# Sixteen raw weight buffers and four high ones in order of use, loads held until the first gather, one weight split moved ahead of the result copy, and a contiguous gated tile

## The chip, the cores and the metric

The kernel runs on one core of a Trainium2 chip, in one launch. The metric is the device time of one execution in microseconds. Three runs of the kernel before took 1229.41, 1229.84 and 1231.94 us; their median is 1229.84 us. The engines are TensorE (PE for its matmuls, PEld for its weight loads), VectorE (DVE), ScalarE (ACT), GpSimd (POOL) and SyncE (SP). SyncE here only issues transfers; GpSimd issues the gathers and the scatters.

## The reference, cut to what matters

One transformer block over 512 tokens of width 1024, all in fp32: three token mixers (dilated attention, a gated recurrence, attention over a memory), then a mixture of experts. The change touches the second half alone: the router, the shared expert's end and the 64 routed experts. Each token takes 8 experts.

```
u = rmsnorm(x, ffn_norm_g[layer]).reshape(B * S, D)
s = jax.nn.sigmoid(u @ w_router)                      # 512 x 64
...                                                   # groups, top 8 of 64, weights w
def swiglu(t, w_up, w_down):
    gate, up = split_cols(t @ w_up, (w_down.shape[0], w_down.shape[0]))
    return (jax.nn.silu(gate) * up) @ w_down
...                                                   # for every expert e, over its tokens tok
y = swiglu(u_pad[tok], w_exp_up[e], w_exp_down[e])    # 1024 x 512, then 256 x 1024
acc.at[tok].add(y * w_of_slot[slots][:, None])
...
x = x + routed + shared
```

## The kernel before, in words

Everything is held in one SBUF tensor, `arena`, whose regions are used again and again under other names. In the trace most operands are therefore called `arena`; `high`, `low`, `gatheredT` and `hidT` are views with a name of their own, and `bank` is PSUM.

**An expert.** An expert has 3 MB of weights, in three blocks of 1 MB (128 x 2048 fp32): two of `w_exp_up` and one of `w_exp_down`. Products are made to nearly fp32 precision in three passes: each operand is split into a high part (rounded to fp32r) and a low part (what is left), and high x high, low x high and high x low are added up (`products`, L1448 to L1452). So each block that a transfer brings goes through ScalarE (`high`, L792: copy the raw block into one of `high_part`) and VectorE (`low`, L1353: raw minus high, written in the place of the raw block). TensorE then uses the pair, and increments `block_used`. Before, there are 12 slots for raw and low (`SLOTS`) and 6 for high (`HIGHS`). Block q of a turn of four experts (`TURN`) lies in slot q modulo 12, and blocks are loaded and split expert by expert: up, up, down, up, up, down.

**An expert on each engine.** GpSimd gathers the expert's rows of `u_rows` (96 at most, L516) into a staging tile of two halves, four experts ahead in its program, and each gather waits until TensorE has transposed the tile's former rows (`gT_done`). TensorE transposes them (L1833), ScalarE and VectorE split them into `gatheredT` (L554, L1363), TensorE multiplies with the two up blocks (24 matmuls), ScalarE takes the tanh of the gate half (L812), and VectorE makes the gated tile `hid` in two steps (`hidden`, L1366: L1370, then L1373). L1373 reads its inputs at a stride of two and writes each half of `hid` by itself, so that TensorE's transpose (L1854) reads contiguous columns. The transposed tile is split into `hidT`, multiplied with the down block (12 matmuls), and copied out of PSUM by ScalarE (`result`, L815, two copies). GpSimd scatters the rows and adds them onto the output in HBM (L524). TensorE's own order in an expert n is: transpose `hid` of n, up of n+1, transpose the tokens of n+2, down of n.

**What sets the order.** Each engine's program is written out by hand, with semaphores between them. `expert` on ScalarE (L823) is: split `hidT` of n, `result` of n-1, high of two blocks, tanh of n+1, tokens of n+2, high of the third block. SyncE issues the loads in the order of the experts (`load_expert_block`, L437), each behind a wait for its slot. Two waits in GpSimd's queue matter: a scatter waits for its own result (`y_ready`) and for the scatter before it to have landed (`added`), since both may add to one row. `result` of m waits for the scatter of m-2 (L819), which frees its half of `y_out`.

```
            def scatter(e, r):
                wait_pass(y_ready, r, E, e + 1)
                if not isinstance(r, int) or e >= 1:
                    wait_pass(added, r, 16 * E, 16 * e)
...
            def result(n, m, used):
                act.wait_ge(block_used, used)
                if not isinstance(m, int) or m >= 2:
                    act.wait_ge(added, m * 16 - 16)
```

**The start of the experts.** The first blocks are loaded while the shared expert runs, as regions of `arena` come free: six after the output projection, four more (slots 6 to 9) when the shared expert's up products are done (`s_up`), and slots 10 and 11, which are the rows of `x`, when the four stores of `x` plus the shared expert have landed (`out_stored`). After that each load waits for `block_used`.

The four experts of a turn are one body of code: a first turn, a loop, and a last turn. The loop runs over the 14 turns between on TensorE, VectorE and ScalarE, and over 15 on SyncE. A second pass for experts with over 96 tokens stands behind a branch.

## Time and profile before

| | |
|---|---|
| median of three runs | 1229.84 us |
| the profiled execution's own time | 1231.59 us |
| its span, first to last instruction | 1229.3 us |
| granted TensorE clock, mean | 0.984 |
| busy: PE, PEld, DVE, ACT, POOL | 1137.4 (93%), 860.9 (70%), 900.8 (73%), 723.1 (59%), 222.1 (18%) us |
| DMA, all transfers | 285.58 MB, mean 232 GB/s |

Busy time is a sum over the whole span, and the span has two halves of different kinds. The routed experts run from about 576 us to the end. The page's second part, 40 slices of 30.7 us each, shows them: from slice 20 on the DMA digit is 9, at 355 to 378 GB/s, where the half before has 1 to 4 in most slices. The time that TensorE is busy says little there, because its digit is 9 in both halves.

### The profile page before, as it was taken

The page shows a single profiled execution, that of the slowest core. Times are in us where ns is not written, and L with a number is a line of the kernel's source. Part 1 is how long each engine was busy: PE and PEld are TensorE (multiplying, and loading weights), DVE is VectorE, ACT ScalarE, POOL GpSimd, SP SyncE. Part 2 cuts the span into 40 slices and gives each one's busy share as a digit, 9 for nine tenths or more (in the row PEclk, how much of TensorE's full clock was granted, in tenths as well). Part 3 has the DMA queues.
Part 4 walks back from the last instruction along what each step waited for, and adds up shares of the span by engine and source line. Part 5 has one row for each costly group of instructions (what it writes and reads, how often), then busy time and mean ns, then how long its engine had stood idle before and what let it go on. Part 6 is the DMA issues. An engine that isn't in the chain of part 4 may idle for free.

```text
span 1229.3 us, 16284 instructions
## 1 busy us (share of the span) xinstructions
PE 1137.4 (93%) x5707; PEld 860.9 (70%) x5707; DVE 900.8 (73%) x1133; ACT 723.1 (59%) x926; POOL 222.1 (18%) x145
## 2 busy tenths in 40 slices
PE   4999998989999899998999999999999999999893
PEld 3699997766777688774666666666666667666662
DVE  4585468544433576578899999998989899999881
ACT  7543343333333422413788888888878788888781
POOL 1000000000000000001232333333433233333421
PEclk9999999999999999999999999999999999999997
DMA  6413232221212234267899999999999999999982
GB/s 214 134 53 103 86 95 69 69 69 34 68 35 68 81 120 137 86 257 272 298 355 362 366 364 369 367 362 369 375 370 368 370 366 378 373 377 362 370 291 33
DMA packets 74495, 285.58 MB, mean 232 GB/s; under 512 B 10868, under 2 KB 33416, under 8 KB 49620
## 3 DMA queue, kind: packets, MB, share of 16 engines
q1 hardware_dynamic: 59716, 251.16, 54.2%
q0 software_dynamic: 14736, 33.87, 11.6%
q8 instruction: 24, 0.39, 0.1%
q14 instruction: 19, 0.16, 0.0%
HBM read 272.39 MB, written 29.38 MB: 245 GB/s over the span
## 4 chain that ended last, share of the span: by engine, by line
PE 58%; DMA 14%; DVE 12%; ACT 7%; issue 7%; SPq 0%; DVEq 0%; POOL 0%; ACTq 0%; POOLq 0%
PE bank L1452 47%; DMA arena<-in_w_exp_up_dram 12%; DVE low L1356 4%; ACT high L554 4%; DVE gatheredT L1363 2%; PE bank L1620 2%; DMA out_dram<-arena 2%; ACT arena L554 2%; PE bank L1647 2%; PE bank L1833 1%; PE bank L1531 1%; PE bank L1778 1%; PE bank L1632 1%; DVE arena L1370 1%; DMA arena<-in_x_dram 1%
## 5 line engine op out<-in xcount | busy, mean ns | idle before, releaser
L1356 DVE TENSOR_TENSOR low<-arena,high 128x2048 fp32r<-128x2048 f32 x192 | 435.3, 2287 | 51.7 <-ACT high L554 51.5
L554 ACT ACTIVATE high<-arena 128x2048 fp32r<-128x2048 f32 x192 | 363.9, 1918 | 23.0 <-DMA arena<-in_w_exp_up_dram 22.2
L1452 PE MATMUL bank<-high,gatheredT 128*96 128x512 f32 x1024 | 327.0, 401 | 19.2 <-DVE gatheredT L1363 17.9
L516 POOL DMA_INDIRECT arena<-u_rows,arena x64 | 103.3, 1614 | 742.1 <-DVE arena L1351 563.5
L1452 PEld LDWEIGHTS bank<-high,gatheredT 128*96 128x96 f32 x1024 | 161.5, 163 | 93.2 <-issue 23.9
L1452 PE MATMUL bank<-low,gatheredT 128*96 128x512 f32 x512 | 203.2, 397 | 0.0
L1452 PE MATMUL bank<-high,hidT 128*96 128x512 f32 x512 | 163.6, 401 | 1.5 <-ACT arena L554 1.5
L524 POOL DMA_INDIRECT out_dram<-arena x64 | 112.7, 1761 | 250.1 <-DMA out_dram<-arena 148.5
L1452 PE MATMUL bank<-hT_high,front_split 128*128 128x512 f32 x448 | 146.4, 409 | 0.8 <-DVE hT_low L892 0.8
L554 ACT ACTIVATE arena<-bank 96x512 f32<-96x512 f32 (+4 forms) x217 | 107.7, 533 | 62.9 <-PE bank L1452 28.3
L1452 PEld LDWEIGHTS bank<-low,gatheredT 128*96 128x96 f32 x512 | 83.4, 163 | 36.5
L1452 PEld LDWEIGHTS bank<-hT_high,front_split 128*128 128x128 f32 x448 | 83.2, 193 | 28.7 <-issue 11.5
L1452 PE MATMUL bank<-low,hidT 128*96 128x512 f32 x256 | 101.0, 395 | 0.0
L886 DVE TENSOR_TENSOR front_split<-arena,front_split 128x2048 fp32r<-128x2048 f32 (+2 forms) x26 | 52.1, 2004 | 63.4 <-ACT front_split L554 63.3
L1452 PEld LDWEIGHTS bank<-high,hidT 128*96 128x96 f32 x512 | 78.0, 162 | 28.7 <-issue 1.6
L1452 PE MATMUL bank<-front_split,hT_high 128*128 128x384 f32 (+1 forms) x384 | 96.0, 332 | 0.0
L1452 PE MATMUL bank<-hT_low,front_split 128*128 128x512 f32 x224 | 89.1, 398 | 0.0
L554 ACT ACTIVATE front_split<-arena 128x2048 fp32r<-128x2048 f32 (+2 forms) x36 | 62.6, 1738 | 27.4 <-PE bank L1452 16.7
L1452 PEld LDWEIGHTS bank<-front_split,hT_high 128*128 128x128 f32 x384 | 68.8, 191 | 0.9 <-issue 0.3
L554 ACT ACTIVATE gatheredT<-bank 128x384 fp32r<-128x384 f32 x128 | 55.8, 488 | 21.8 <-PE bank L1833 21.8
L1363 DVE TENSOR_TENSOR gatheredT<-bank,gatheredT 128x384 fp32r<-128x384 f32 x128 | 64.7, 545 | 1.5 <-ACT gatheredT L554 1.5
L1452 PE MATMUL bank<-front_split,hT_low 128*128 128x384 f32 (+1 forms) x192 | 63.1, 329 | 0.0
(253 smaller groups left out, 1402.5 us busy)
## 6 DMA issues: line engine op xcount, KB each, us to landing
arena<-in_w_exp_up_dram SPq DMA_DIRECT2D x128, 1024.0 KB, 22.7
arena<-in_w_exp_down_dram SPq DMA_DIRECT2D x64, 1024.0 KB, 18.8
arena<-in_w_in_dram SPq DMA_DIRECT2D x14, 1024.0 KB, 5.4
arena<-in_w_in_dram SPq DMA_DIRECT2D x10, 768.0 KB, 4.4
arena<-in_w_branches_dram SPq DMA_DIRECT2D x4, 1024.0 KB, 5.0
arena<-in_w_out_dram SPq DMA_DIRECT2D x4, 1024.0 KB, 5.0
arena<-in_x_dram SPq DMA_DIRECT2D x4, 512.0 KB, 5.5
arena<-in_w_mem_kv_dram SPq DMA_DIRECT2D x2, 1024.0 KB, 5.0
```

The lines of the kernel that those rows point to most:

```text
L516: pool.indirect_dma_start(gathered[0:ROWS, e % 2, :], None, u_dram, bass.IndirectOffsetOnAxis(ap=index[0:ROWS, e:e + 1], axis=0), bounds_c ...
L524: pool.indirect_dma_start(out_rows, bass.IndirectOffsetOnAxis(ap=index[0:ROWS, e:e + 1], axis=0), y_out[0:ROWS, e % 2, :], None, bounds_ch ...
L554: return nc.scalar.activation(o, i, ACT.Copy, **kw)
L886: v.tensor_tensor(low_part, raw_block(w), high_part.bitcast(F32), ALU.subtract).then_inc(front_low, 1)
L1356: v.tensor_tensor(low_part[q % SLOTS], raw[q % SLOTS], high_part[q % HIGHS].bitcast(F32), ALU.subtract).then_inc(low_done, 1)
L1363: v.tensor_tensor(parts[:, 1], view(ps[half][:, 0:4 * ROWS], 4, ROWS), parts[:, 0].bitcast(F32), ALU.subtract).then_inc(gT_low, 1)
L1370: v.scalar_tensor_tensor(e_act[0:ROWS, n % 2, :], e_tanh[0:ROWS, n % 2, :], 1.0, bank[0:ROWS, 0:FH], ALU.add, ALU.mult).then_inc(act_ready, 1)
L1452: ins = mm(bank, left[a], right[b], start=first and q == 0, stop=last and q == 2)
L1531: last = mm(ps[4 + q][:, z * P:(z + 1) * P], left[rows, b, c * P:(c + 1) * P], right[rows, b, c * P:(c + 1) * P], start=True, stop=True)
L1620: mm(ps[2 + j % 2][:, 0:keys], qkT[rows, 0, t * P:(t + 1) * P], qkT[rows, 1, 0:keys], start=True, stop=True).then_inc(qk_done, 1)
L1632: last = tr(ps[4][:, kt * P:(kt + 1) * P], probs[:, j % 2, kt * P:(kt + 1) * P], ident)
L1647: last = mm(ps[j % 2][:, 0:HD], probsT[:, j % 2, kt * P:(kt + 1) * P], values, start=kt == 0, stop=kt == tiles - 1)
```

## The change

- **Buffers.** 16 slots for raw and low instead of 12, 4 for high instead of 6. The two regions of the former fifth and sixth high buffer become slots 10 and 11, two more in `ib` become slots 12 and 13, and the rows of `x` become slots 14 and 15. Small tiles of the router that lay in `ib` move elsewhere (`place`, `w_high`, `w_low`, `token_of`).
- **Order of use.** Blocks are numbered, loaded and split in the order in which TensorE uses them: up of n+1 stands ahead of down of n (`up_at`, `down_at`). One load waits for the block that was in its slot (`block_used`), and every high now also waits for the block that used its high buffer four blocks ago.
- **Loads and stores at the start.** Slots 10 and 11 wait for `set_done`, 12 and 13 for `folded`, 14 for the first two stores of `x`, 15 for the other two. The stores stand behind block 10 (two of them) and block 13 (two). Behind the first two stores SyncE waits for the first gather to land.
- **ScalarE.** In `expert` the high of up block 0 of n+2 stands ahead of `result`, the high of its block 1 behind it; the down block's high is the last.
- **The gated tile.** The second step of `hidden` is contiguous in all its operands, and TensorE's transpose reads `hid` at a stride of two.
- **Turns.** `TURN` is 16 instead of 4, since 16 slots and 4 high buffers have to come round within a turn: the first turn, the loop's body and the last turn each hold 16 experts of code. The loop's body runs twice on TensorE, VectorE and ScalarE, and three times on SyncE.

```
-TURN = 4
+DEAL = 4
+TURN = 16
-SLOTS, HIGHS = 12, 6
-LEAD = 5
+SLOTS, HIGHS = 16, 4
+ROUNDS = BLOCKS * TURN // SLOTS
...
+def up_at(n, j, first=False):
+    return j if first and n == 0 else BLOCKS * n - 1 + j
+def down_at(n, last=False):
+    return BLOCKS * n + (2 if last and n == TURN - 1 else 4)
...
-        slot_at = [ring_at + 2048 * n for n in (2, 3, 4, 5, 0, 1)] + [gates_at + 2048 * n for n in (0, 1, 4, 5)] + [x_at, x_at + 2048]
+        slot_at = ([ring_at + 2048 * n for n in (2, 3, 4, 5, 0, 1)] + [gates_at + 2048 * n for n in (0, 1, 4, 5, 2, 3)]
+                   + [ib_at, ib_at + 2048, x_at, x_at + 2048])
...
+            def load(src, k, u):
+                s = k % SLOTS
+                if not isinstance(u, int) or k >= SLOTS:
+                    sp.wait_ge(block_used, u + (k - SLOTS + 1))
...
+                elif s < 12:
+                    sp.wait_ge(set_done, 1)
+                elif s < 14:
+                    sp.wait_ge(folded, 1)
                 else:
-                    sp.wait_ge(out_stored, 16 * NT)
+                    sp.wait_ge(out_stored[s - 14], 16 * NT // 2)
+                sp.dma_start(raw[s].rearrange("p k n -> p (k n)"), src).then_inc(raw_in[s], 16)
+            def store_rows(k, u):
+                if isinstance(u, int) and k in (10, 13):
+                    for t in (0, 1) if k == 10 else (2, 3):
+                        sp.wait_ge(out_ready, t + 1)
+                        sp.dma_start(out[0, t * P:(t + 1) * P, :], x_tok[:, t, :]).then_inc(out_stored[t // 2], 16)
+                    if k == 10:
+                        sp.wait_ge(gather_in[0], 16)
...
                 act.wait_ge(hidT_done, m + 1)
                 copy(hidT[:, n % 2, 0, :], ps[3][:, 0:2 * ROWS]).then_inc(hidT_high, 1)
+                if ups:
+                    high(up_at(n + 2, 0), u, round0)
                 if not start:
-                    result(n + 1, m - 1, u + 2)
-                for j in range(min(blocks, 2)):
-                    high(q + j, u + (LEAD + j), round0)
+                    result(n + 1, m - 1, u + (down_at(n - 1) + 1))
+                if ups:
+                    high(up_at(n + 2, 1), u, round0)
...
-                v.scalar_tensor_tensor(hid[0:ROWS, n % 2, :].rearrange("p (k f) -> p f k", k=2),
-                                       e_act[0:ROWS, n % 2, :].rearrange("p (f k) -> p f k", k=2), slot_w[0:ROWS, one(e)],
-                                       bank[0:ROWS, FH:2 * FH].rearrange("p (f k) -> p f k", k=2), ALU.mult,
-                                       ALU.mult).then_inc(hid_ready, 1)
+                v.scalar_tensor_tensor(hid[0:ROWS, n % 2, :], e_act[0:ROWS, n % 2, :], slot_w[0:ROWS, one(e)],
+                                       bank[0:ROWS, FH:2 * FH], ALU.mult, ALU.mult).then_inc(hid_ready, 1)
...
-                    last = tr(ps[3][:, f * ROWS:(f + 1) * ROWS], hid[0:ROWS, n % 2, f * P:(f + 1) * P], ident[0:ROWS, 0:ROWS])
+                    last = tr(ps[3][:, f * ROWS:(f + 1) * ROWS], hid[0:ROWS, n % 2, :].rearrange("p (f k) -> p k f", k=2)[:, f, :],
+                              ident[0:ROWS, 0:ROWS])
```

SyncE's queue at the start of the experts, before. Loads are `in_w_exp_...`, the stores of the shared expert's rows are `out_dram`:

```order
L454 DMA arena<-in_w_exp_up_dram 128x2048 [waits s_up] x2
L456 DMA arena<-in_w_exp_down_dram 128x2048 [waits s_up]
L454 DMA arena<-in_w_exp_up_dram 128x2048 [waits s_up]
L464 DMA out_dram<-arena 128x1024 [waits out_ready] x4
L454 DMA arena<-in_w_exp_up_dram 128x2048 [waits out_stored]
L456 DMA arena<-in_w_exp_down_dram 128x2048 [waits out_stored]
```

And in the changed kernel:

```order
L458 DMA arena<-in_w_exp_up_dram 128x2048 [waits s_up]
L458 DMA arena<-in_w_exp_down_dram 128x2048 [waits s_up]
L458 DMA arena<-in_w_exp_up_dram 128x2048 [waits s_up] x2
L458 DMA arena<-in_w_exp_down_dram 128x2048 [waits set_done]
L464 DMA out_dram<-arena 128x1024 [waits out_ready] x2
L458 DMA arena<-in_w_exp_up_dram 128x2048 [waits set_done,gather_in0]
L458 DMA arena<-in_w_exp_up_dram 128x2048 [waits folded]
L458 DMA arena<-in_w_exp_down_dram 128x2048 [waits folded]
L464 DMA out_dram<-arena 128x1024 [waits out_ready] x2
L458 DMA arena<-in_w_exp_up_dram 128x2048 [waits out_stored0]
L458 DMA arena<-in_w_exp_up_dram 128x2048 [waits out_stored1]
```

Ten loads stand ahead of the first store before, eleven now. Three more stand between the stores, and only the sixteenth waits for the last store.

ScalarE's queue in one expert of the first turn, before (`high` is a weight block's split, the two copies from `bank` of 96x512 are the result, 96x256 is the tanh):

```order
L554 ACTIVATE hidT_92<-bank3 128x192
L554 ACTIVATE arena<-bank4 96x512
L554 ACTIVATE arena<-bank6 96x512
L554 ACTIVATE high2_87<-arena 128x2048
L554 ACTIVATE high3_88<-arena 128x2048
L812 ACTIVATE arena<-bank2 96x256
```

And in the changed kernel:

```order
L568 ACTIVATE hidT_94<-bank3 128x192
L568 ACTIVATE high0_89<-arena 128x2048
L568 ACTIVATE arena<-bank4 96x512
L568 ACTIVATE arena<-bank6 96x512
L568 ACTIVATE high1_90<-arena 128x2048
L828 ACTIVATE arena<-bank2 96x256
```

One block's split has moved ahead of the two copies of the result.

## Rows read from the trace of the kernel before

**Rows 1.** Windows: us, busy (x) of PE, PEld, DVE, ACT, POOL, PEclk, DMA share, GB/s.

```profile
555.00:580.00 25.00, 21.07 (x86) 11.60 (x85) 20.59 (x53) 6.96 (x9) 4.17 (x3) 0.98 0.71 275
580.00:605.00 25.00, 23.32 (x111) 16.27 (x110) 20.91 (x18) 16.88 (x20) 4.12 (x4) 0.95 0.76 276
607.18:818.50 211.32, 206.86 (x1014) 146.57 (x1012) 194.30 (x178) 175.14 (x199) 68.06 (x44) 1.00 1.03 363
818.50:1176.13 357.63, 340.88 (x1658) 239.47 (x1656) 320.03 (x290) 288.43 (x325) 130.06 (x72) 1.00 1.02 370
1180.00:1205.00 25.00, 23.45 (x112) 16.13 (x111) 20.91 (x19) 16.29 (x19) 5.12 (x3) 1.00 0.65 195
```

**Rows 2.** Waits of 605 to 1205 us: engine line <- releaser, us, times, longest.

```profile
POOL out_dram L524 <- DMA out_dram<-arena: 143.9, 32, 8.7
POOL out_dram L524 <- ACT arena L554: 82.4, 27, 5.3
ACT high L554 <- DMA arena<-in_w_exp_up_dram: 22.2, 22, 2.4
```

**Rows 3.** GpSimd's timeline: start, us, what [idle before it <- releaser].

```profile
570.58 2.23 POOL L516 DMA_INDIRECT arena<-u_rows,arena  x1 [563.51 <-DVE arena L1351]
...
609.80 1.44 POOL L524 DMA_INDIRECT out_dram<-arena  x1 [3.15 <-DMA out_dram<-arena]
...
1181.72 1.52 POOL L524 DMA_INDIRECT out_dram<-arena  x1 [6.45 <-DMA out_dram<-arena]
...
1213.76 1.42 POOL L524 DMA_INDIRECT out_dram<-arena  x1 [4.63 <-DMA out_dram<-arena]
```

**Rows 4.** Scatters issued at 605 to 800, 800 to 1175 and 1185 to 1229 us.

```profile
L524 POOL DMA_INDIRECT out_dram<-arena x20: 1442/1442/1792, 609.8 to 792.3; - x20
DMA to landing us min/median/max: 8.1/8.7/9.6
L524 POOL DMA_INDIRECT out_dram<-arena x38: 1442/1816/3447, 802.0 to 1171.7; - x38
DMA to landing us min/median/max: 8.4/9.0/10.5
...
DMA to landing us min/median/max: 5.2/5.4/5.6
```

**Rows 5.** The chain that ended last, 600 to 610 us: start, us, what.

```profile
600.34 8.65 DMA out_dram<-arena
...
609.03 0.77 issue
```

**Rows 6.** SyncE's timeline at the experts' start, and its last load.

```profile
564.03 12.14 SPq L464 DMA_DIRECT2D out_dram<-arena  x4
578.83 0.34 SPq L454 DMA_DIRECT2D arena<-in_w_exp_up_dram  x1
...
1176.46 0.33 SPq L456 DMA_DIRECT2D arena<-in_w_exp_down_dram  x1
```

**Rows 7.** ScalarE, VectorE and TensorE in one expert, 674 to 685 us.

```profile
675.00 1.07 ACT L554 ACTIVATE arena<-bank 96x512 f32<-96x512 f32 x2
675.96 3.72 ACT L554 ACTIVATE high<-arena 128x2048 fp32r<-128x2048 f32 x2
...
682.88 0.69 DVE L1373 SCALAR_TENSOR_TENSOR arena<-arena,bank 96x256 f32<-96x256 f32 x1 [0.16 <-DVE arena L1370]
...
674.85 0.69 PE L1452 MATMUL bank<-high,gatheredT 128*96 128x512 f32 x2
684.55 0.70 PE L1452 MATMUL bank<-high,gatheredT 128*96 128x512 f32 x2 [0.28 <-DVE gatheredT L1363]
```

**Rows 8.** Lines 1370 and 1854: duration ns min/median/max, first and last start.

```profile
L1370 DVE SCALAR_TENSOR_TENSOR arena<-arena,bank x64: 404/409/416, 586.2 to 1203.5; 96x256 f32<-96x256 f32 x64
L1854 PEld LDWEIGHTS bank<-arena x128: 137/142/146, 587.4 to 1205.6; 96*128 96x128 f32 x128
```

**Rows 9.** The page's third part: queue, kind, packets, MB, share of 16 engines.

```profile
q8 instruction: 24, 0.39, 0.1%
```

More of the change, by code:

```diff
@@ L121, in take @@
             return offset
[L123 removed]
+        square_at = take(6, P)
+        square = at(square_at, 6, P)
         ident, flip, counting, before, ones, level = (square[:, n, :] for n in range(6))
@@ L180, in build @@
         s_hid = at(qa_at, NT, FH)
-        ro = [at(ib_at + n * 256, NT, E) for n in range(16)]
-        (score, choice, masked, masked2, picked, weight, place) = ro[0:7]
+        (score, choice, masked, masked2, picked, weight) = [at(ib_at + n * 256, NT, E) for n in range(6)]
+        place = at(square_at + P, NT, E)
         router_bias = at(ib_at + 11 * 256, E)
@@ new lines, in load_turn, with load_pass @@
+            def load_turn(e, n, u, first=False):
+                for j in range(2):
+                    load(up_src[:, e, j, :], up_at(n, j, first), u)
+                    store_rows(up_at(n, j, first), u)
+                if not first or n:
+                    load(dn_src[:, e - 1, :], down_at(n - 1), u)
+                    store_rows(down_at(n - 1), u)
+            def load_pass(u0):
+                for n in range(TURN):
+                    load_turn(n, n, u0, True)
+                with sp.Fori(1, E // TURN) as g:
+                    for n in range(TURN):
+                        load_turn(g * TURN + n, n, u0 + g * (BLOCKS * TURN))
+                load(dn_src[:, E - 1, :], BLOCKS * TURN - 1, u0 + BLOCKS * (E - TURN))
@@ L474, in _ @@
                     with sp.If(fullest > r * ROWS):
[L475 to L479 removed]
+                        sp.wait_ge(index_ready, r + 1)
+                        load_pass(r * (BLOCKS * E))
         @block.gpsimd
@@ L535, in expert_pass @@
                     if isinstance(r, int) and e == 0:
-                        pool.wait_ge(out_stored, 16 * NT)
+                        for h in range(2):
+                            pool.wait_ge(out_stored[h], 16 * NT // 2)
                     scatter(e, r)
@@ L1232, in shared @@
                 read_deal(0)
-                low(1, 1)
+                low(1, 0)
                 take_down(2)
```

180 lines of the change are left out of this document (77 added, 103 removed).

## The prediction, made before the changed kernel was run

> **What bounds the kernel now.** I read the windows first. From 607 us to 1176 us TensorE is busy for 206.86 of 211.32 us and then for 340.88 of 357.63 us, at a granted clock of 1.00 (its upper level, 2.4 GHz), and the DMA share is 1.02 to 1.03 throughout [rows 1]. Two resources are full at once, so I looked at what each of them delivers per expert. The first stretch holds 22 experts, 9.61 us each, with 9.40 us of TensorE's work. The second holds 36 (the transpose of expert 24 to that of 60), 9.93 us each, with 9.47 us of it. So TensorE loses 0.2 us per expert first, and 0.5 us later.
>
> The list of waits says what it loses them to. In the later part ScalarE waits for an up block from HBM: 22 waits, 22.2 us in all [rows 2]. The loads are late there. They were not at first: the slots give a lead, and a load queue that needs more than 9.61 us per expert eats it up. In a tuned pipeline like this the last load's landing therefore counts. The load of the last block is issued at 1176.46 us [rows 6], and the window of 1180 to 1205 us still has a share of 0.65, that is 25 x 0.65 / 1.02 = 16 us of full transfers, so the loads end near 1196 us.
>
> GpSimd shows a third queue. It is idle for most of the time, but its largest wait there is of a scatter for the scatter before it: 32 times, 143.9 us [rows 2]. One scatter takes 8.7 us to land in the first stretch and 9.0 in the later one, 5.4 us once the loads are over [rows 4], and the next is issued 0.8 us after a landing (0.77 us of issue in the chain [rows 5]). Back to back, the 58 scatters from the one at 609.80 us on would need 20 x 9.5 + 38 x 9.8 = 562.4 us. They took 1181.72 - 609.80 = 571.9 us [rows 3]. The scatters run back to back with 9.5 us of slack in all. A chain like that ends the kernel whatever TensorE does, and the last one here is a scatter, at 1213.76 us.
>
> **The change part by part.**
>
> The start of the loads. DMA share is 0.71 at 555 to 580 us and 0.76 at 580 to 605 us, against 1.02 when full [rows 1]: 7.6 and 6.4 us of every engine's time stand empty. The reason is in SyncE's rows: after the tenth load nothing but four stores (2 MB) is issued until 578.83 us, since slots 10 and 11 are the rows being stored [rows 6], and the load after those two waits for a used block. Now block 10 goes ahead of the stores, and from the first gather's landing near 576 us (issued at 570.58 us [rows 3]) blocks 11 to 14 go out without a wait. A block is 1.05 MB, 2.9 us at 363 GB/s. I count 2.9 us for block 10, 2.8 us for the start at 576 instead of 578.8 us, and all 6.4 us of the second window: 12 us. Block 15 waits for the last two stores, behind three loads in the queue; while it waits, block 14 and those are still being served, so I take nothing off. The bounds are 6 us (the hold costs most of it) and 14 us (no hole left). The loads then end near 1184 us.
>
> The hold itself removes nothing that shows before: the first gather landed before 576 us with an idle load queue. It keeps it so.
>
> Code. Three turns of 16 experts are more code than three of 4. Code came as 24 transfers of 0.39 MB in all on queue 8 [rows 9], 16 KB each. The longest program is TensorE's, with some 5300 instructions on the path that is run; it grows by 3400, so some 16 such transfers, 0.26 MB. All engines together I put at 0.35 MB, 1 us at 363 GB/s. The loads end at 1185 us, 11 us earlier.
>
> The order of use. Before, ScalarE splits blocks in the order in which they are loaded, and it still does, with the second block of three ahead of the tanh in both. So a late load hits it at the same place, and I count nothing.
>
> Four high buffers. In an expert the first split needs the buffer of the previous down block, used just before the transpose; the second that of the first up block, used near 2.8 us after TensorE begins (12 of its 36 matmuls; the 36 and the transposes take 9.7 - 0.28 = 9.42 us [rows 7]). With the `hidT` copy, a split and the result ahead of it, 1.9 + 1.07 us without the first, the second split could not start earlier anyway [rows 7]. Its buffer costs nothing, as long as the result stands between; without that cover it would cost ScalarE 0.9 us per expert, 2.8 less 1.9. The third needs a block that is long used.
>
> The split ahead of the result, and the gated tile. VectorE's row of one expert ends a chain: split, low, gated tile, `gatheredT`, then TensorE, which waited 0.28 us for it [rows 7]. The contiguous step should take what the first step of the same size and operands takes, 0.41 us, instead of 0.69 [rows 7, 8]: 0.28 us off the chain. The earlier first split lets VectorE start its first low sooner, another 0.3 us at most. That covers the 0.2 us of idle time: TensorE could go at 9.42 us per expert instead of 9.61. The transpose's weight load, 142 ns [rows 8], now reads at a stride of two. If it slowed as the strided step did (0.69 / 0.41), two of them would add 0.2 us per expert; at best they add nothing. Over the 22 unhindered experts the net is 0 to 4 us earlier, and none of it reaches the end while the loads and scatters decide. On the sum I count 0.
>
> The price is the result's copy: it comes one split later, 3.72 / 2 = 1.9 us [rows 7]. The scatter's issue follows it. Behind the waiting scatter on GpSimd stands only the next gather, which is needed two experts later. The delay shifts all scatters once by 1.9 us; expert 1 comes about 0.9 us earlier, because its blocks are split before the first down block, so the chain starts at 610.8 instead of 609.80 us.
>
> The scatters' chain, then. From 610.8 us the 58 take at least 562.4 us, to 1173 us. I give them 568, between that floor and the 571.9 us of before, because the waits for late loads, which cost them the slack, begin later: 1179 us. From there one more at 9.4 us including its issue (the loads are ending at 1185 us), then three at 5.4 + 0.8 = 6.2 us: the last is issued at 1207.0 us instead of 1213.76. The loads' own end would allow the last result 11 us earlier, near 1201 us, so the scatters decide. The gain is 6.8 us. The profiled execution took 1231.59 us with a span of 1229.3, so it would be 1224.8; it lies 1.75 us above the median of 1229.84. On the median I predict 1223 us.
>
> How a longer load queue acts on the scatters is the term with the widest bounds. The scatters' median was 8.7 us in the first stretch and 9.0 in the later, when more loads were outstanding, both at a full share [rows 4]. No row has the queue filled with more than 12. I take no change, as the share is full in both; the low bound is -0.1 us each, the high +0.3 us each, the difference between the stretches: -6 to +17 us. By the Trainium skill ("DMA: Bandwidth & Descriptors", section "Queues, rings and completion order") each DMA engine goes round robin between its queue rows, a packet at a time, so loads queued behind each other would not lengthen a scatter; these rows agree to 0.3 us, and the sum would stay as it is.
>
> **The rivals.**
>
> A: the scatters give way. Their landing time is set by the load traffic beside them, and the row of 5.4 us without loads shows how far it can fall. If the slack of 9.5 us goes entirely, the chain reaches 1173 us and the loads' end at 1185 us decides: gain 11 to 12 us, 1218 us. For it: TensorE's busy share leaves room. Against: 32 waits for the scatter before.
>
> B: nothing moves. The 58 scatters take their 571.9 us again, from a start 1 us later, and win only at the end, where the loads stop sooner: 0 to 2 us, 1229 us. For it: in the stretch of 605 to 800 us they already run back to back, before any load is late.
>
> C, slower: each scatter lands later beside a queue that is always full and deeper. It decides from 6.8 / 58 = 0.12 us per scatter on; at 0.3 us the chain ends 17 us later, 10 us behind now: 1240 us. For it: 8.7 against 9.0 us. Against: the maximum of the first stretch, 9.6 us, already came with few loads outstanding.
>
> D, slower by a stall of code: the loop's body is four times as long, and its back branch comes once on TensorE, VectorE and ScalarE. If the body is gone by then, one fetch stands in the full queue like a gather, up to 9 us, on the engine that feeds the chain: 1229.8 - 6.8 + 9 = 1232 us. No row of before shows a stall at a back branch, with short bodies. The Trainium skill ("Runtime: NRT & Kernel Launch", section "Instruction fetch mechanics") says that a taken branch outside the resident pages stalls for a fetch; no run here shows it yet. By its sizes (2048 instructions for TensorE, 512 for the others) TensorE's body of 1578 would stay, while ScalarE's 276 and VectorE's 243 may straddle a third page, and the time would be the 1232 us of this rival.
>
> That the change does not do what it says is small: if the strided transpose cost 0.2 us, TensorE would stay at 9.6 us, still under the scatters' 9.8.
>
> **How the numbers follow.** Forecast (1223 us) 0.47, A (1218) 0.19, B (1229) 0.18, C (1240) 0.10, D (1232) 0.06. A difference of 0.2%, 2.5 us, is about what a measurement of this kernel can tell from none. Faster than that: nearly all of the first two, and a fifth of B: 0.69. Within it: most of B and a part of D: 0.15. Slower: C, the rest of D and what I have not thought of: 0.16. The range takes A's best, 1230 - 14, and reaches up over D: 1216 to 1233 us.
>
> **What would show it.** DMA share at 580 to 605 us near 1.0, the last load issued 9 to 12 us earlier, L1373's second step near 410 ns, the first scatter near 601 us, and scatters landing in 8.7 to 9.0 us. The gain would stand in the last scatter's issue, near 1207 us. Wrong: scatters at 9.2 us or more, a hole of several us at expert 32 on one engine, or TensorE waiting for a high buffer. If TensorE still shows the waits for up blocks from 800 us on, the lead was not there.

## The result and the profile after

The changed kernel takes 1243.59 us in the median of 4 runs (1239.8 to 1243.94), the kernel before 1229.62 (1228.5 to 1231.94) beside it. The ratio is 1.0105, interval 1.0080 to 1.0129: slower by 1%. I had predicted 1223 us and a range up to 1233. The profiled execution took 1239.8 us with a span of 1238.0, 3.8 us under that median. Medians and ranges below are of all runs of a kernel, while a ratio compares only the runs within 1.5% of that kernel's fastest with the kernel before run beside them.

The loads did what I had counted on. Windows of the changed kernel (columns as in [rows 1]):

```profile
580.00:605.00 25.00, 23.42 (x114) 16.64 (x113) 21.20 (x21) 17.28 (x21) 6.78 (x4) 0.97 1.02 382
655.00:905.00 250.00, 236.71 (x1143) 167.96 (x1142) 216.88 (x199) 197.75 (x225) 96.33 (x49) 0.99 1.02 368
1180.00:1205.00 25.00, 24.75 (x125) 17.83 (x124) 23.05 (x22) 21.54 (x25) 15.73 (x6) 1.00 0.37 67
```

The hole at 580 to 605 us is closed (1.02 for 0.76), and at 1180 to 1205 us the share is 0.37 for 0.65. The last load lands at 1182.6 us, 13 us before the 1196.0 us of the kernel before. SyncE issues its last two with the group below, which ends at 1167.98 us; the last one goes out 8.8 us before the 1176.46 us of [rows 6]:

```profile
1164.33 3.65 SPq L458 DMA_DIRECT2D arena<-in_w_exp_down_dram  x2
```

GpSimd's timeline, which answers to [rows 3]:

```profile
610.71 1.44 POOL L537 DMA_INDIRECT out_dram<-arena  x1 [5.83 <-DMA out_dram<-arena]
...
1196.83 2.62 POOL L537 DMA_INDIRECT out_dram<-arena  x1 [2.05 <-DMA out_dram<-arena]
...
1222.75 1.42 POOL L537 DMA_INDIRECT out_dram<-arena  x1 [5.65 <-DMA out_dram<-arena]
```

The second scatter starts at 610.71 us, where I had 610.8. The one 58 later starts at 1196.83, where I had 1179; before it was 1181.72. The last starts 9.0 us later than before. The scatters' landing over the stretches of [rows 4] (the issue is part of it):

```profile
L537 POOL DMA_INDIRECT out_dram<-arena x19: 1442/1451/3272, 610.7 to 795.2; - x19
DMA to landing us min/median/max: 8.2/9.7/10.8
L537 POOL DMA_INDIRECT out_dram<-arena x37: 1442/1793/3272, 804.6 to 1167.9; - x37
DMA to landing us min/median/max: 5.8/9.2/11.6
```

In the first stretch the median went from 8.7 to 9.7 us, in the second from 9.0 to 9.2. Part of it is GpSimd's own time in the instruction. Grouped over 605 to 1180 us, the kernel before and then the changed one (xcount | busy, mean ns of one | idle before <- releasers):

```profile
L524 POOL DMA_INDIRECT out_dram<-arena x58 | 103.3, 1780 | 214.7 <-DMA out_dram<-arena 128.7 <-ACT arena L554 77.2 <-issue 8.7
```

```profile
L537 POOL DMA_INDIRECT out_dram<-arena x56 | 116.1, 2073 | 329.6 <-DMA out_dram<-arena 315.8 <-ACT arena L568 7.0 <-issue 6.7
```

That is 0.29 us more per scatter. The chain of the 58 scatters took 1196.83 - 610.71 = 586.1 us for 571.9, 14 us more. Over scatters 1 to 56 the issue adds 18 us and the rest of the landing 5 (0.32 and 0.09 us each, from the table of the next section). Against that stand 4 us, since scatters hardly wait for their result any more, and 5 us at the end, where the loads stop sooner. And the waits of 605 to 1205 us, which answer to [rows 2], have a kind that was not there:

```profile
POOL out_dram L537 <- DMA out_dram<-arena: 331.3, 58, 7.4
DVE low L1373 <- ACT high L568: 67.6, 68, 3.2
ACT arena L568 <- DMA out_dram<-arena: 35.4, 30, 2.7
PEld bank L1847 <- DMA arena<-u_rows,arena: 34.3, 29, 2.7
```

TensorE's token transposes (`PEld bank L1847`) wait 29 times for a gather. ScalarE's result copies (`arena L568`) wait 30 times for a scatter to land. They have run a whole expert ahead, and both buffers of `y_out` are full. What that does stands in the timelines at 732 to 746 us, GpSimd, then ScalarE, then VectorE (start, us):

```profile
733.11 3.05 POOL L537 DMA_INDIRECT out_dram<-arena  x1 [6.75 <-issue]
744.39 1.44 POOL L537 DMA_INDIRECT out_dram<-arena  x1 [5.93 <-DMA out_dram<-arena]
...
740.22 1.91 ACT L568 ACTIVATE high<-arena 128x2048 fp32r<-128x2048 f32 x1
743.61 1.08 ACT L568 ACTIVATE arena<-bank 96x512 f32<-96x512 f32 x2 [1.48 <-DMA out_dram<-arena]
...
732.56 2.28 DVE L1373 TENSOR_TENSOR low<-arena,high 128x2048 fp32r<-128x2048 f32 x1
742.20 2.29 DVE L1373 TENSOR_TENSOR low<-arena,high 128x2048 fp32r<-128x2048 f32 x1
746.52 2.29 DVE L1373 TENSOR_TENSOR low<-arena,high 128x2048 fp32r<-128x2048 f32 x1 [2.04 <-ACT high L568]
```

The scatter at 733.11 us meets a low pass that began at 732.56 and ends at 734.84; its issue takes 3.05 us and ends 1.3 us after the pass. The one at 744.39 us meets a pass that ends 0.1 us later, and takes 1.44 us. The result at 743.61 us waited 1.48 us for the same landing that releases the scatter at 744.39. In the kernel before no result copy waits for a landing.

All scatters 1 to 56 of both traces follow one rule. If a low pass began at least 0.1 us before the issue and has more than 0.2 us to go, the issue ends 1.31 to 1.33 us after the pass; if none is under way, or one begins later, the issue takes 1.44 us. A pass was under way at 38 of the 56 before and at 36 in the changed kernel, so it is not that more scatters meet one. They meet it earlier in its course: 2 found more than 1 us of it left before, 21 in the changed kernel.

The Trainium skill ("SBUF — State Buffer", section "SBUF: two separate sides") states that VectorE and GpSimd share one pair of ports under an exclusive lock held for a whole instruction, and that a VectorE instruction with two inputs in SBUF takes it against a GpSimd instruction that reads SBUF. That a DMA issued from GpSimd waits for its descriptors it says of VectorE instructions in a 2-port mode. The low pass has two inputs in SBUF, and these rows show the wait beside it: 3.05 against 1.44 us. I had not weighed this rule.

### The profile page after: what moved, and what is told of

It is laid out like the page before. It is cut to its first block, busy times and chain, and to the rows that moved or that the text cites. A ratio compares the mean times of both kernels' runs of the same rounds, so it can differ in the third digit from the quotient of the medians.

```text
span 1238.0 us, 15884 instructions
## 1 busy us (share of the span) xinstructions
PE 1140.3 (92%) x5707; PEld 866.0 (70%) x5707; DVE 892.9 (72%) x1133; ACT 723.8 (58%) x926; POOL 258.3 (21%) x145
## 2 busy tenths in 40 slices
DMA packets 74519, 285.90 MB, mean 231 GB/s; under 512 B 10868, under 2 KB 33416, under 8 KB 49620
## 4 chain that ended last, share of the span: by engine, by line
DMA 47%; PE 38%; DVE 6%; issue 5%; ACT 2%; POOL 0%; SPq 0%; POOLq 0%; DVEq 0%; ACTq 0%
DMA out_dram<-arena 46%; PE bank L1466 29%; PE bank L1634 2%; PE bank L1661 2%; PE bank L1545 1%; PE bank L1646 1%; DMA arena<-in_x_dram 1%; ACT front_split L568 1%; ACT arena L568 1%; DVE front_split L903 1%; DVE arena L1001 0%; DMA arena<-u_rows,arena 0%; DVE hT_low L909 0%; DMA arena<-in_w_in_dram 0%; PE bank L1624 0%
## 5 line engine op out<-in xcount | busy, mean ns | idle before, releaser
L568 ACT ACTIVATE high<-arena 128x2048 fp32r<-128x2048 f32 x192 | 367.2, 1913 | 0.7 <-PE bank L1466 0.5
L529 POOL DMA_INDIRECT arena<-u_rows,arena x64 | 117.9, 1842 | 600.5 <-DVE arena L1368 561.7
L537 POOL DMA_INDIRECT out_dram<-arena x64 | 134.4, 2099 | 364.4 <-DMA out_dram<-arena 341.3
L1466 PE MATMUL bank<-high,hidT 128*96 128x512 f32 x512 | 168.3, 411 | 1.9 <-DVE hidT L1398 1.9
L568 ACT ACTIVATE arena<-bank 96x512 f32<-96x512 f32 (+4 forms) x217 | 107.9, 531 | 104.5 <-DMA out_dram<-arena 35.4
L1466 PE MATMUL bank<-hT_high,front_split 128*128 128x512 f32 x448 | 143.9, 402 | 0.8 <-DVE hT_low L909 0.8
L568 ACT ACTIVATE gatheredT<-bank 128x384 fp32r<-128x384 f32 x128 | 55.9, 489 | 38.4 <-PE bank L1847 38.4
L568 ACT ACTIVATE front_split<-arena 128x2048 fp32r<-128x2048 f32 (+2 forms) x36 | 62.6, 1738 | 25.6 <-PE bank L1466 16.7
L1847 PEld LDWEIGHTS bank<-arena 96*128 96x128 f32 x512 | 47.4, 140 | 42.1 <-DMA arena<-u_rows,arena 34.3
L1847 PE MATMUL bank<-arena 96*128 96x96 f32 x512 | 54.1, 248 | 23.9 <-DMA arena<-u_rows,arena 23.9
```

What stands on the lines that cost most here:

```text
L529: pool.indirect_dma_start(gathered[0:ROWS, e % 2, :], None, u_dram, bass.IndirectOffsetOnAxis(ap=index[0:ROWS, e:e + 1], axis=0), bounds_c ...
L537: pool.indirect_dma_start(out_rows, bass.IndirectOffsetOnAxis(ap=index[0:ROWS, e:e + 1], axis=0), y_out[0:ROWS, e % 2, :], None, bounds_ch ...
L568: return nc.scalar.activation(o, i, ACT.Copy, **kw)
L1466: ins = mm(bank, left[a], right[b], start=first and q == 0, stop=last and q == 2)
L1847: last = tr(ps[k // 4][:, (k % 4) * ROWS:(k % 4 + 1) * ROWS], gathered[0:ROWS, n % 2, k * P:(k + 1) * P], ident[0:ROWS, 0:ROWS])
```

## The experiments

"issue" is GpSimd's time in a scatter and "rest" its landing less the issue, both means over scatters 1 to 56. "lap" is the first scatter that starts on the same landing as the next expert's result copy, that is, the copies are a whole expert ahead. "reads" are 16 KB packets of code on queue 8 between 655 and 905, 905 and 1075, 1075 and 1180 us. All but the times are of the profiled execution.

| kernel | loop | us, median (range) | reads | issue | rest | lap | ScalarE's waits for a landing |
|---|---|---|---|---|---|---|---|
| before | 4 | 1230 (1225 to 1239) | 0, 0, 0 | 1.75 | 7.17 | none | 0 |
| b_split_first | 4 | 1230.7 (1226.5 to 1250.4) | 0, 0, 0 | 1.84 | 7.16 | none | 0 |
| b_contiguous | 4 | 1229.2 (1225.9 to 1231.9) | 0, 0, 0 | 1.87 | 7.16 | none | 0 |
| a_small_plain | 4 | 1226.0 (1222.0 to 1227.7) | 0, 0, 0 | 1.86 | 7.12 | none | 0 |
| a_small | 4 | 1243.5 (1226.3 to 1253.9) | 1, 0, 0 | 2.11 | 7.27 | 9 | 47 |
| b_turn8 | 8 | 1235.0 (1229.2 to 1243.3) | 3, 0, 1 | 2.03 | 7.27 | 14 | 40 |
| b_turn16 | 16 | 1250.6 (1246.6 to 1255.5) | 9, 0, 4 | 1.96 | 7.51 | 14 | 35 |
| a_small_turn16 | 16 | 1242.3 (1239.6 to 1246.8) | 9, 0, 4 | 1.95 | 7.35 | 17 | 35 |
| after | 16 | 1243.6 (1239.8 to 1243.9) | 9, 0, 4 | 2.07 | 7.26 | 10 | 30 |

The row "before" takes all its 100 runs in this study for the time. In the four kernels at the top the result copy starts 1 to 9 us ahead of its scatter to the end of the loads, 1.4 to 3 us for most experts before, 4 to 6 us in b_split_first and about 7 us in b_contiguous and a_small_plain, and never a whole expert. The trace of a_small is that of the slowest of its ten runs.

In what follows, P is the theory that VectorE's low pass holds up the issue, Q that the fuller load queue lengthens the landing, C that the longer loop does it, R that TensorE's faster pace does, L that the result copies' lead over the scatters does, and G that the gather's bytes do. This C is not the prediction's rival C, whose reason is Q's.

### Is it the split ahead of the result, the buffers, or the low pass?

**a_result_first**: `result` ahead of both high passes again.

```
-                if ups:
-                    high(up_at(n + 2, 0), u, round0)
                 if not start:
                     result(n + 1, m - 1, u + (down_at(n - 1) + 1))
                 if ups:
+                    high(up_at(n + 2, 0), u, round0)
                     high(up_at(n + 2, 1), u, round0)
```

> The changed kernel with the result's copies ahead of both splits again, all else as changed. Theory P (VectorE's low pass, which reads two SBUF operands, holds up GpSimd while it issues a scatter; the split ahead of the result moved a low pass over the moment after a scatter lands): the scatter's issue on GpSimd falls from 2.07 us back to 1.75 us or less, landing from 9.34 to 9.0 us or less, time 1222 to 1230 us. Theory Q (the fuller load queue makes each scatter land later) and theory C (the longer code): no effect, issue stays at 2.07 us, time 1240 to 1244 us.

1241.68 us, ratio 1.0083 (1.0057 to 1.0109), mean issue 1.96 us. That is at most 2 us of the 14, within the two intervals; theory P's 1222 to 1230 us is missed.

**b_split_first**: the kernel before with one high pass ahead of the result.

> The kernel before with one part of the change alone: one weight split ahead of the result's copies. Theory P: this part alone costs the time, scatter issue 2.0 us or more, landing 9.3 us, time 1240 to 1248 us, since the loads bring no gain at the end. Theories Q and C: 1229 to 1232 us, as before.

1230.68 us, ratio 1.0013 (0.9977 to 1.0049), but from 1226.5 to 1250.4 in 10 runs; three of them lie above all 100 runs of the kernel before. The moved split alone does not make the kernel slow, as theory P had it; it makes it able to be.

**a_small**: the changed kernel with `SLOTS, HIGHS = 12, 6` and `TURN = 4`; all four stores stand behind block 10, the last two of them behind the first gather.

> The changed kernel with 12 slots, 6 high buffers and turns of 4, still in order of use, with the split ahead of the result and the contiguous tile; slots 10 and 11 are the regions that are free when the deal is folded, all stores stand behind block 10 and the last two behind the first gather. Theory P: still slow, scatter issue about 2.0 us, time 1238 to 1244 us. Theory Q (16 slots fill the queue): landing back to 9.0 us, time near 1230 us. Theory C (code of 16 experts per turn): near 1230 us too.

1226.3 to 1253.9 us in 10 runs, median 1243.5, ratio 1.0010 (0.9976 to 1.0044). In the profiled one (1253.9) 47 result copies waited for a landing. No theory expected so wide a spread of one kernel. With a loop of 4 the other parts of the change can therefore still be as slow as the whole, in some runs.

**a_low2**: each low pass as two instructions of half the size.

> The changed kernel with each low pass in two instructions of half the size. Theory P: GpSimd waits for the end of one instruction at most, 1.15 us instead of 2.29, so the mean issue of a scatter falls by about 0.3 us to 1.75 us; VectorE gets three more instructions per expert, some 0.2 us, which it has room for. Time 1228 to 1236 us. Theories Q and C: the same or slower than 1243 us.

1242.55 us, ratio 1.0093 (1.0067 to 1.0118). The gather's mean issue fell from 1.87 to 1.50 us, the scatter's stayed at 2.10, where theory P expected 1.75. The second half begins at once: at 698.54 us it runs from 0.05 us before the scatter's start to 1.17 us behind it, and the issue takes 2.49 us, again 1.32 us more.

**a_no_low**: the low pass writes 4 columns in place of 512 and TensorE takes the high block twice, so the low part of the weights is left out.

> The changed kernel in which VectorE's low pass of an expert block writes 4 columns of 512, and TensorE takes the high block twice in its place (so the low part of the weights is left out). ScalarE, TensorE's instructions, loads, gathers and scatters stay. Theory P: the scatter's issue falls from 2.1 to about 1.44 us and each of 56 scatters with it, so 37 us at most off the chain; the loads' end at 1182 then decides, 1208 to 1216 us. Theory G (gather beside scatter): the issue is only part of it; landing without issue stays at 7.2 us, and the kernel gains nothing but 0 to 10 us, 1230 to 1240 us.

1222.42 us (1219.95 to 1226.31), ratio 0.9951 (0.9927 to 0.9975). The scatters of 605 to 1180 us, columns as above:

```profile
L537 POOL DMA_INDIRECT out_dram<-arena x59 | 85.2, 1443 | 408.6 <-DMA out_dram<-arena 246.0 <-ACT arena L568 147.4 <-issue 15.3
```

All 59 are issued in 1.44 us, the rest stays 7.28. So the stretch is the low pass's, shown by taking it away. The gain is 21 us, less than my 27 to 35: the scatters now wait 147.4 us for ScalarE, whose high passes wait 70 times and 73.7 us for an up block.

**a_no_gather**: from expert 8 on a gather fetches 64 words a row in place of 1024; the rest of the row stays stale.

> The changed kernel in which the gathers of expert 8 and on fetch 64 words a row in place of 1024 (the rest of the row stays stale, so this part of the result is left out); the descriptors stay 96. Theory G (the gather's bytes, issued right behind the scatter's on the same queue, stretch scatter and gather): a scatter lands in 8.3 us or less, at least 1 us sooner, and the kernel takes 1212 to 1222 us. Theory P (VectorE stretches the issue): the issue stays 2.1 us, the landing at least 9.0 us, the kernel at least 1232 us.

1226.58 us (1219.8 to 1234.0), ratio 0.9975 (0.9948 to 1.0002), issue 2.03 us, median landing 9.0. Neither theory: the page has 272.21 MB moved for 285.90 MB, 13.7 MB less, and 17 us went with them, with the stretch still there. The rest of the landing fell from 7.26 to 7.08 us, which is 10 us over 56 scatters. So the gather's bytes beside a scatter do count, by less than theory G's 1 us.

### Is it TensorE's pace?

**a_strided** (the gated tile and its transposes as before, the rest changed) and **b_contiguous** (the reverse):

> The changed kernel with the gated tile and its transposes strided as before; all else of the change stays. Theory R (pace): the contiguous tile lets TensorE run ahead of the scatters at 9.2-9.3 us an expert, so that scatter follows scatter with no gap and the gather is issued right behind each; strided again, it goes back to a gap before the scatter, a scatter issue of about 1.76 us and 1226 to 1232 us. Theory P (VectorE's low pass, two operands in SBUF, is under way when GpSimd issues the scatter, since scatter now follows landing at once): the strided tile changes nothing in that, issue 2.1 us and 1240 to 1244 us. Theory C (the longer loop, TURN 16): 1240 to 1244 us too.

> The kernel before with the contiguous gated tile and strided transpose alone. Theory R (pace): TensorE goes 0.1 to 0.3 us faster an expert and overtakes the scatters: scatter upon scatter, 1236 to 1250 us. Theory P and C: VectorE, buffers and loop are as before, the second gated step 0.28 us shorter gives 1226 to 1231 us, scatter issue about 1.76 us.

1244.13 us, ratio 1.0113 (1.0083 to 1.0142), and 1229.18 us, ratio 1.0006 (0.9991 to 1.0021). The tile is worth nothing that shows either way; theory R is refuted.

**a_paced**, **a_rf_paced**, **a_rf_paced_half**: more transposes of the hidden tile, in the last two with the result first.

```
-                for f in range(2):
+                for f in (0, 1, 0, 1):      # a_rf_paced_half: (0, 0, 1)
```

> The changed kernel in which TensorE transposes the hidden tile of each expert twice (two transposes of about 0.25 us more an expert, same data, 0.5 us an expert in all). Theory L (lead): in the changed kernel the result copies run so far ahead of the scatters that from about expert 12 each waits for the same landing as the scatter does; VectorE's low pass then starts just as GpSimd issues the scatter and stretches every other issue to about 3 us. A slower TensorE keeps the result 1 to 3 us ahead of its scatter as in the kernel before, the mean issue falls from 2.1 to 1.9 us or less, and the kernel, with more work on TensorE, gets faster than the 1243.6 us of the changed kernel: 1226 to 1238 us. Theory C (longer code) and theory Q (fuller load queue beside the scatters): nothing is gained by it, 1243 us or more, up to 1275 us if TensorE sets the end.

> As the one above (hidden transposes twice), and with the result's copies ahead of both high passes, as in the kernel before. Theory L: with the result first, ScalarE's next high and so VectorE's next low come after the scatter's issue; lead 1 to 3 us, mean issue 1.5 to 1.8 us, 1222 to 1232 us. Theories C and Q: 1241 us or more.

> Result first, and one transpose more an expert in place of two (0.25 us). Theory L: TensorE at about 9.5 us an expert is close to a scatter at 1.44 + 7.2 + 0.8 = 9.44 us; between 1218 us (lead stays small) and 1240 us (lead grows to a full expert within the 64). Theories C and Q: 1241 us or more.

1243.56 (1235.3 to 1249.4), 1250.77 (1249.7 to 1251.7) and 1235.88 us (1224.8 to 1243.6), ratios 1.0107, 1.0166 and 1.0032. The first two miss theory L's forecasts. I wanted to slow TensorE by 0.5 us per expert and got 0.2: the rest stood in its waits. Result copies still came to wait for landings (24, 28 and 31 times). As a test of a slower TensorE it is inconclusive; a_rf_paced also read more code, 47 packets on queue 8 for 38, nine of them between 905 and 1051 us.

### Is it the longer loop?

**b_turn16**: the kernel before, its buffers, order and tile unchanged, its loop written out 16 times.

```
-TURN = 4
+TURN = 16
+DEAL = 4
...
-                if not isinstance(e, int):
-                    sp.wait_ge(block_used, u0 + (BLOCKS + 2 - SLOTS if j == 2 else j - SLOTS + (n == 0)))
+                if not isinstance(e, int) or n >= 4:
+                    sp.wait_ge(block_used, u0 + (BLOCKS + 2 - SLOTS if j == 2 else j - SLOTS + (n == 0 or n == 4)))
...
+            for n in range(4, TURN):
+                load_expert(n, n, BLOCKS * n)
```

> The kernel before with its expert loop written out 16 times in place of 4 (buffers, order and tile as before): the longer code alone. Theory C (code is fetched beside the scatters and stretches them): 1236 to 1245 us. Theories L and Q: as before, 1227 to 1233 us.

1250.61 us (1246.6 to 1255.5), ratio 1.0176 (1.0113 to 1.0238). One constant, with the loads' waits and counters that follow from it, makes the kernel before slower than the changed kernel, and slower than theory C's 1236 to 1245 us. The page's third part gives as much code read in it as in the changed kernel, against the 24 packets of [rows 9], and its waits of 605 to 1205 us have the changed kernel's marks:

```profile
q8 instruction: 38, 0.62, 0.2%
```

```profile
POOL out_dram L527 <- DMA out_dram<-arena: 339.0, 57, 8.7
...
ACT arena L557 <- DMA out_dram<-arena: 37.7, 35, 2.8
```

**b_turn8**: the same with 8.

> The kernel before with its expert loop written out 8 times. With 4 there is no 16 KB read of code between 655 and 1180 us, with 16 one every 25 to 30 us. Theory C (the reads slow the scatters they meet by 0.4 to 0.7 us, the result copies get ahead until they wait for the landing, and then VectorE stretches the issue): if a loop of 8 is read again each time, 1236 to 1250 us with reads of 16 KB all along; if it stays in the engines' buffers, 1227 to 1233 us and no such reads. Theory L alone (nothing to do with code): 1227 to 1233 us in both cases.

1234.96 us (1229.2 to 1243.3), ratio 1.0030 (0.9997 to 1.0062), so the median's 5 us are not clear of noise, though the times stand in the order 4, 8, 16. The profiled run took 1241.1. It reads a block of 16 KB at 730 us, and the next at 1161. Its waits of 750 to 1150 us:

```profile
POOL out_dram L527 <- DMA out_dram<-arena: 211.8, 39, 7.0
...
ACT arena L557 <- DMA out_dram<-arena: 23.3, 35, 2.0
```

35 result copies of some 40 wait for a landing in a stretch in which no block of code is read. Once there, the kernel stays there.

**b_spare**: the kernel before with 30 more DMAs of 16 KB.

```
+                    if n % 2:
+                        sp.dma_start(spare_dram[n // 2:n // 2 + 1, :], io["x"][0].rearrange("(a b) d -> a (b d)", b=4)[0:1, :]).then_inc(spare_in, 16)
```

> The kernel before, loop of 4, with one more DMA of 16 KB every second expert from SyncE (30 in all, from x to a spare tensor that nobody reads). Theory C-dma (what counts of a read of code is a large packet on a DMA engine that the scatter also uses): 1236 to 1250 us, and scatters with such a packet in flight take 0.4 to 0.7 us more. Theory C-supply (the engines wait for their code): 1227 to 1233 us.

1234.40 us (1232.1 to 1237.9), ratio 1.0034 (1.0012 to 1.0055), rest 7.19 us, no result copy at a landing. Inconclusive, for the trace shows that it was no copy of a code read: each came as 16 packets of 1 KB over the engines, while a read of code is one packet of 16 KB that takes 1.08 us on one.

### What is left of the change with a short loop?

**a_small_plain**: order of use and contiguous tile, 12 and 6 buffers, loop of 4, result first, nothing held.

```
-TURN = 16
+TURN = 4
...
-SLOTS, HIGHS = 16, 4
+SLOTS, HIGHS = 12, 6
-                if isinstance(u, int) and k in (10, 13):
+                if isinstance(u, int) and k == 9:
...
-                    if k == 10:
-                        sp.wait_ge(gather_in[0], 16)
```

> The changed kernel's order of use and contiguous gated tile with 12 raw and 6 high buffers, loop of 4, result ahead of both highs and no load held. Theory C: without the long loop 1225 to 1231 us. If order of use itself costs (another theory): 1236 us or more.

1226.04 us (1222.0 to 1227.7), ratio 0.9958 (0.9940 to 0.9976): faster than both kernels. Its waits of 605 to 1205 us have no result copy at a landing. Its loads at 580 to 605 us, and its last scatter:

```profile
580.00:605.00 25.00, 23.41 (x118) 16.80 (x117) 21.06 (x22) 18.69 (x23) 6.11 (x4) 1.00 1.01 347
```

```profile
1207.22 1.42 POOL L537 DMA_INDIRECT out_dram<-arena  x1 [5.31 <-DMA out_dram<-arena]
```

6.5 us earlier than before, in a run of 1225.3 us.

**a_small_turn16** (the same, loop of 16) and **a_small_split_first** (the same, loop of 4, one high pass ahead of the result):

> a_small_plain (order of use, contiguous tile, 12 raw and 6 high buffers, result first, no load held; 1226 us) with its loop written out 16 times in place of 4. Theory C: reads of 16 KB of code all along up to about 900 us, result copies that wait for the landing from expert 10 to 15 on, 1240 to 1252 us. If the longer loop hurts only together with the order of before: 1224 to 1230 us.

> a_small_plain with one high pass ahead of the result's copies, as in the changed kernel. If the split ahead is what made runs of a_small fall into 1242 to 1254 us: a median of 1230 us or more with some runs above 1240. If it was the held load and the first scatter's later start: 1224 to 1228 us in nearly all runs.

1242.28 us, ratio 1.0100 (1.0042 to 1.0158): the longer loop costs 16 us here, and the kernel is then within 2 us of the changed one. And 1234.17 us (1223.8 to 1246.5), ratio 1.0023 (0.9986 to 1.0060): with the split ahead some runs fall back, without it none of 10 did.

**a_no_hold**: the changed kernel without SyncE's wait for the first gather.

> The changed kernel without SyncE's wait for the first gather. Theory C: the loop is still written out 16 times, so 1238 to 1246 us; the first scatters come 0 to 4 us later beside the fuller queue. If the held loads are what sets the phase of the scatters: below 1234 us.

1249.90 us (1243.2 to 1252.6), ratio 1.0127 (1.0087 to 1.0167), 6 us more than the changed kernel and more than either forecast. Its first scatter:

```profile
607.14 2.34 POOL L535 DMA_INDIRECT out_dram<-arena  x1 [4.64 <-ACT arena L566]
```

That is 6.8 us after the 600.34 us of [rows 5]; the changed kernel's first starts at 600.39 us. The two intervals overlap. So with this loop holding the loads shows no cost.

## Why the prediction was wrong

**Loads: right.** The eighteenth load lands 12 us earlier and the last 13 us earlier, for my 12 and 11, with a share of 1.02 where I had asked for near 1.0. The waits for an up block (22.2 us, [rows 2]) are gone. Four high buffers, as predicted, cost nothing that shows: from 605 to 1205 us ScalarE is idle before a high pass for 0.4 us in all:

```profile
L568 ACT ACTIVATE high<-arena 128x2048 fp32r<-128x2048 f32 x181 | 346.3, 1913 | 0.4 <-PE bank L1466 0.2
```

**Gated tile: half right, and of no weight.** The second step went from 0.69 us [rows 7] to 0.48, not to the 0.41 of the first step. The strided transpose's weight load went from 142 ns [rows 8] to 196:

```profile
L1390 DVE SCALAR_TENSOR_TENSOR arena<-arena,bank x64: 475/477/480, 585.4 to 1211.9; 96x256 f32<-96x256 f32 x64
L1869 PEld LDWEIGHTS bank<-arena x128: 194/196/224, 586.0 to 1213.6; 96*128 96x128 f32 x128
```

**The step that failed** is "From 610.8 us the 58 take at least 562.4 us, to 1173 us. I give them 568". They took 586.1 us, above even the 571.9 us of before. The last scatter came at 1222.75 us for my 1207.0, and the profiled run at 1239.8 for 1224.8: the whole miss of that run. The median misses by 5.6 us more, because the profiled run lay 1.75 us above the median before and 3.8 us below it now.

What I took as a floor, the medians of before, was no floor. Taken with means, a step of the kernel before is 1.75 us of issue, 7.17 of rest and 0.84 to the next start, 9.76 us, and waits for a result hold the starts back by 4 us in all, where I had 9.5 of slack. And the issue's share of it held only for the phase that the engines had in that kernel, in which a scatter met the last part of a low pass or none. In the changed kernel it meets more of the pass, and the mean issue is 2.07 us. With the result copy about 7 us ahead the mean issue is 1.86, and in the kernels with a lap 1.95 to 2.11. I had its parts on the page: the issue's minimum, median and maximum of 1442, 1816 and 3447 ns stand in [rows 4], and I used the median without asking what made the maximum. Had I, VectorE's rows beside it would have shown the low pass, and GpSimd's waits (27 times on ScalarE, 32 times on the scatter before, [rows 2]) how near to each other the two came.

**Code** I counted as bytes (1 us of traffic) and as a stall at the back branch (rival D, 0.06). No stall shows: TensorE goes through experts 2 to 12 at 9.2 to 9.8 us each, as fast as I had hoped. The transfers themselves came as I had them, 14 more for my 16. Yet the loop's length alone is enough to undo the change: it costs 21 us in the kernel before and 16 in the small design, and without it, with the result first and nothing held, the order of use gains 4 us. It is not the only way there, as a_small shows. The Trainium skill ("Runtime: NRT & Kernel Launch", section "Instruction fetch mechanics") says that a straight run crosses a block of code with its fetch mostly hidden. For the engine that runs it these traces agree, with the 9.2 to 9.8 us above. Scatters beside it are another matter: the 15 whose time from issue to landing overlaps such a read took 7.75 us after their issue, the other 41 took 7.08; in b_turn16 it is 7.98 and 7.34, in a_small_turn16 7.94 and 7.13, in a_no_hold only 7.40 and 7.12.

**Where the time of the long loop stands.** In the two pairs that differ in the loop of 16 alone, most of it is not in the issue. From before to b_turn16 the issue adds 12 us over 56 scatters and the rest of the landing 19; from a_small_plain to a_small_turn16 they add 5 and 13. In the changed kernel it is 18 and 5. So the low pass explains most of what the changed kernel lost on its chain, and the smaller part of what the long loop alone costs. The 15 scatters that meet a read would come to some 10 to 12 us in each of the three kernels, by the differences above.

**The rivals.** C came nearest in time (1240 us), through landings, as it said, of 9.7 us for 8.7 in the first stretch. Its reason, the fuller load queue, is not it: b_turn16 and a_small_turn16 have 12 slots, and the one is slower than the changed kernel, the other within 2 us of it. A and B are out.

**What stays open.** The chain from the low pass to a longer issue is shown by removal and by the 1.32 us. That a loop of 16 makes the kernel slow is shown by two pairs of kernels. How it does so is argued, not shown: scatters that meet a code read land later, the result copies gain on them, and once they have a lead of one expert both are released by the same landing, which puts a low pass at the scatter's start again and again. That the reads delay the scatters is a coincidence in time alone; a copy of a code read as one packet of 16 KB was not made. In b_turn16 the scatters that meet none also take 7.34 us for 7.14, and that is not explained. What tips a_small, which reads no block of code between 657 and 1180 us, in some runs and not in others is open too.

## What to carry to other kernels

Read the spread of a duration, not its median alone: a GpSimd DMA whose issue goes from 1.4 to 3.4 us is meeting something, and a change that shifts the phase of the engines moves the mean. In a kernel whose buffers fill up, ask how far each producer runs ahead and what happens when two waits come to end on one event: there the following experts may all be slower, though no single instruction is. And price a longer loop by running it alone, before the buffers that need it.

## What the runs showed of the hardware that I had not expected

- GpSimd's indirect DMA beside a VectorE pass with two SBUF operands took up to 3.3 us to issue in the changed kernel between 605 and 1180 us instead of 1.44, and its issue ended 1.32 us after the pass; without the pass all 59 take 1.44 us, and gathers 0.98 for 1.87. Two passes of half the length, one right behind the other, did not shorten the scatter's issue (2.10 us).
- With a loop body of 4 experts no 16 KB of code is read between 657 us and the loop's end. One of 16 is read in its first turn and hardly in its second: none or one such read between 905 and 1075 us in eleven of the twelve kernels with it, but nine in a_rf_paced.
- One program can spread over 24 to 28 us with the same code and data: 1226.5 to 1250.4 (b_split_first) and 1226.3 to 1253.9 us (a_small), at a mean granted clock of 0.98 to 0.99 in every run.
- With the loads over (from 1182.6 us on), a scatter still takes 4.7 to 8.4 us to land, and the last four steps of the chain take 5.8 to 7.1 us each.
